# A gated delta rule on one core: inverse in packed blocks of 64, unnormalized q and k, four units of v ahead of the norm

## What is computed

```
proj = rmsnorm(x, n_mix_pre) @ w_in                 # q, k, v, z and gates of the delta rule; v of a retention
qkv  = silu(causal_depthwise_conv(concat(qa, ka, va), conv_a))       # 4 taps
qa   = l2norm(qa) * A_DK ** -0.5 ;  ka = l2norm(ka)
beta = sigmoid(beta_logit) ;  g = -exp(a_log) * softplus(a_dt + dt_bias)
lower = where(strict, (beta * k) @ k.T * decay, 0)
t_inv = inverse of (I + lower)                      # unit lower triangular, one for a chunk and head
u, w  = t_inv @ (v * beta), t_inv @ (k * beta * exp(g_cum))
o     = ...                                         # two chunks, a state of 128x256 between them
oa    = rmsnorm(o, norm_a) * silu(z)
```

## Time and profile before

| | us |
|---|---|
| median of 3 runs (1486.3 to 1490.52) | 1490.06 |
| the profiled execution | 1490.92 |
| its span, first to last instruction | 1489.4 |
| start of the layer to the first decay of head 0 | 606.9 to 646.4 |
| laps 0 to 6 | 646.4 to 975.5 |
| gate matmul with head 7 | 975.5 to 1026.1 |

### The profile page before, as it was taken

The page is one execution under the profiler, slowest core; times in us unless marked ns, Lnnn a source line. Parts: engine busy times, 40 slices in busy tenths (PEclk is TensorE's granted clock), DMA queues, the critical chain, the costliest instruction groups (busy, mean ns, idle before and its releaser), DMA issues.

```text
span 1489.4 us, 23158 instructions
## 1 busy us (share of the span) xinstructions
PE 1376.1 (92%) x9500; PEld 1249.6 (84%) x9500; DVE 940.4 (63%) x1479; ACT 730.9 (49%) x1284; POOL 89.7 (6%) x153
## 2 busy tenths in 40 slices
PE   6999999998999999868888988888999999799997
...
PEclk9999999999999999979999999999999999999998
...
GB/s 262 170 142 114 176 220 188 182 168 142 84 143 223 179 192 195 107 114 114 86 85 86 85 104 95 85 85 86 226 177 149 172 162 147 144 238 177 191 142 29
DMA packets 34057, 218.48 MB, mean 147 GB/s; under 512 B 4384, under 2 KB 6176, under 8 KB 8480
## 3 DMA queue, kind: packets, MB, share of 16 engines
...
HBM read 215.94 MB, written 1.05 MB: 146 GB/s over the span
## 4 chain that ended last, share of the span: by engine, by line
PE 75%; DVE 13%; ACT 7%; issue 3%; POOL 1%; DMA 0%; ACTq 0%; DVEq 0%; POOLq 0%
PE bank L289 22%; PE bank L290 21%; PE bank L291 21%; DVE sb_w_lo L271 3%; DVE sb_w_lo L269 2%; DVE sb_d_xt L1518 2%; ACT sb_w_hi L261 2%; PE bank L1509 1%; PE bank L1498 1%; POOL sb_small L363 1%; PE bank L708 1%; PE bank L1512 1%; ACT sb_wide L1339 1%; PE bank L397 1%; DVE sb_d_qkv_r L1346 1%
## 5 line engine op out<-in xcount | busy, mean ns | idle before, releaser
L289 PE MATMUL bank<-sb_h_hi,sb_w_hi 128*128 128x256 f32 x1536 | 445.2, 290 | 12.8 <-DVE sb_w_lo L282 7.6
L290 PE MATMUL bank<-sb_h_lo,sb_w_hi 128*128 128x256 f32 x1536 | 433.5, 282 | 0.0
L291 PE MATMUL bank<-sb_h_hi,sb_w_lo 128*128 128x256 f32 x1536 | 432.9, 282 | 0.0
L269 DVE TENSOR_TENSOR sb_w_lo<-sb_raw,sb_w_hi 128x1024 fp32r<-128x1024 f32 x199 | 242.9, 1221 | 145.4 <-ACT sb_w_hi L261 144.9
L289 PEld LDWEIGHTS bank<-sb_h_hi,sb_w_hi 128*128 128x128 f32 x1536 | 293.7, 191 | 20.1 <-issue 10.8
L290 PEld LDWEIGHTS bank<-sb_h_lo,sb_w_hi 128*128 128x128 f32 x1536 | 293.9, 191 | 2.7 <-issue 1.4
L291 PEld LDWEIGHTS bank<-sb_h_hi,sb_w_lo 128*128 128x128 f32 x1536 | 293.4, 191 | 0.0
L261 ACT CAST sb_w_hi<-sb_raw 128x1024 fp32r<-128x1024 f32 x199 | 208.8, 1049 | 85.2 <-PE bank L291 85.2
L271 DVE TENSOR_TENSOR sb_w_lo<-sb_raw,sb_w_hi 128x1024 fp32r<-128x1024 f32 x199 | 246.3, 1238 | 0.0
L262 ACT CAST sb_w_hi<-sb_raw 128x1024 fp32r<-128x1024 f32 x199 | 209.2, 1051 | 0.0
L289 PE MATMUL bank<-sb_w_hi,sb_h_hi 128*128 128x256 f32 (+1 forms) x544 | 177.9, 327 | 2.8 <-DVE sb_h_lo L431 1.4
...
## 6 DMA issues: line engine op xcount, KB each, us to landing
...
```

What stands on the lines that cost most here:

```text
L269: V.tensor_tensor(w_lo[:, b, 0:HALF], raw[:, r, 0:HALF], w_hi[:, b, 0:HALF].bitcast(F32), ALU.subtract)
L289: T.matmul(out_ap, l_hi, r_hi, start=start, stop=False, **kw)
L290: T.matmul(out_ap, l_hi, r_lo, start=False, stop=False, **kw)
L291: return T.matmul(out_ap, l_lo, r_hi, start=False, stop=stop, **kw)
```

## The change

- **Start.** Four units of v of the retention (RAW_V = 4) come first in the stream and are multiplied with the unnormalized x. Then x is normalized for good (`hn`: 8 instructions on DVE, 4 copies on ACT, 4 subtractions on DVE), and all other projections use the normalized one: `scale_qkv_dve` is gone, the convolution reads PSUM, and the scales `root` are gone elsewhere. The factor for `root` is now found from x times a gain row before the new x is made (`weighted_squares_act`). Laps 4 to 6 therefore have three units instead of four.
- **q and k.** They stay unnormalized. Their squares (ACT, one instruction, in the lap before) are summed by four matmuls with one moving column (`squares_pe`), POOL takes the power and makes scales for rows of `low`, v and k, and the scales of q go into the output's norm. Only k is transposed; `back_qk`, `scale_qk`, `norms` and `turn_low` are gone. q and k of a head have two buffers (`cv_qk`).
- **Inverse.** The two diagonal blocks of 64 of each chunk are inverted together, packed one above the other on the partitions: xt is 128x4x64 instead of 128x4x128, z 128x128 instead of 128x256. Levels 1 to 5 use 64x64 matmuls at rows 0 to 63 and 64 to 127; the corner block is then one step (`corner_a`, `corner_b`, `corner_dve`).
- **Order.** Weight work is issued in halves of a step (6 matmuls), and the small work sits at other places in all four queues.

```diff
     w = i["w_in_2"][0]
+    u += [cols_unit(w, (C_VB + 256 * h, 256)) for h in range(RAW_V)]
...
         def delta_begin_act():
...
+            hi()
+            weighted_squares_act()
...
+            hi(2)
+            keep_v_act(0)
+            keep_v_act(1)
+            row_act(7, 4)
+            for b in range(4):
+                A.wait_ge(hn_done, b + 1)
+                A.copy(h_hi[:, 2 * b:2 * b + 2, :], hn[:, 2 * b:2 * b + 2, :]).then_inc(hn_hi, 1)
+            keep_v_act(2)
             hi()
...
         def delta_begin_dve():
...
+            lo(2)
+            V.wait_ge(delta_in, DELTA_IN)
+            gates_project_dve()
...
+            V.wait_ge(row_done, 5)
+            for k in range(KD):
+                u = bank[AFTER_FFN[k // 2]][:, (k % 2) * S:(k % 2 + 1) * S]
+                ins = V.scalar_tensor_tensor(hn[:, k, :], u, gains[:, 8, k:k + 1], r_row[:], ALU.mult, ALU.mult)
...
+            for b in range(4):
+                V.wait_ge(hn_hi, b + 1)
+                V.tensor_tensor(h_lo[:, 2 * b:2 * b + 2, :], hn[:, 2 * b:2 * b + 2, :],
+                                h_hi[:, 2 * b:2 * b + 2, :].bitcast(F32), ALU.subtract).then_inc(hn_lo, 1)
+            lo(2)
...
+        def squares_pe(hd):
+
+            T.wait_ge(qk_squared, hd + 1)
+            for j in range(4):
+                mm = T.matmul(bank[2][:, 256 + j:257 + j], sq_qk[:, j * P:(j + 1) * P], upper[:, P - 1:P], start=True, stop=True)
+            mm.then_inc(ss_mm, 1)
...
+        def start_own_dve(hd):
+            V.wait_ge(blocks_done, 6 * hd + 1)
+            need(V, zx_mm, 6 * hd)
+            for s, rows in enumerate(HALF_ROWS):
+                V.tensor_tensor(xt[rows, 2:4, :], eye[rows, :].unsqueeze(1).to_broadcast([HB, NT, HB]),
+                                low_b[rows, 0, :, s * HB:(s + 1) * HB], ALU.subtract)
...
         def level_a_pe(hd, b):
-            T.wait_ge(blocks_done, 6 * hd + b)
+            T.wait_ge(blocks_done, 6 * hd + b + 1)
             T.wait_ge(inv, LEVELS * hd + b)
             for t in range(NT):
-                mm = T.matmul(bank[6][:, t * P:(t + 1) * P], low_b[:, b % 2, t, :], xt[:, t, :], start=True, stop=True)
+                for s, rows in enumerate(HALF_ROWS):
+                    mm = T.matmul(bank[6][rows, t * HB:(t + 1) * HB], low_b[rows, b % 2, t, s * HB:(s + 1) * HB], xt[rows, t, :],
+                                  start=True, stop=True)
             mm.then_inc(z_mm, 1)
...
         def delta_first_pe():
-            first_two(unit_d(0, 0), 0, unit_d(0, 1), 1, 20, 4, AFTER_FFN)
+            raw_x = (hr_hi, hr_lo)
+            first_two(unit_d(0, 2), 0, unit_d(1, 2), 1, 20, 4, AFTER_FFN, raw_x, tokens, tokens)
+            for step in range(4):
+                tokens(unit_d(2, 2), 2, step, raw_x)
+            row_pe(7, 5, R0)
+            T.wait_ge(v_ret_done, 1)
+            for step in range(4):
+                tokens(unit_d(3, 2), 0, step, raw_x)
             gates_project_pe()
...
         def delta_first_dve():
+            gates_dve()
+            lo()
             older_dve(0, 0, 1)
...
             older_dve(0, 1, 3)
...
+            new_x_dve()
...
         def delta_pe(hd):
...
+            row_decay_pe(hd)
+            T.wait_ge(v_ret_done, min(A_HEADS, RAW_V + hd))
+            T.wait_ge(conv_d[0], n)
+            head_unit_pe(u, 0, 0, 2)
+            flip_k_pe(hd)
+            squares_pe(hd)
+            products_pe(hd)
             if first:
                 first_values_pe(hd - 1)
...
+            head_unit_pe(u, 0, 6, 8)
+            start_pe(hd)
             if first:
                 outputs_pe(hd - 1)
...
         def delta_act(hd):
...
             silu_act(n, 0)
             level_a_act(hd, 2)
+            squares_qk_act(n)
             if first:
                 store_act(hd - 1)
             newest_act(n, 1)
-            hi()
             level_a_act(hd, 3)
+            if more_v:
+                hi()
             level_a_act(hd, 4)
```

More of the change, by code:

```diff
@@ L60, in constants @@
     out["upper"] = (row <= col).astype(f)
-    out["lower_strict"] = (row > col).astype(f)
     lev = []
-    for b in range(LEVELS):
+    for b in range(LEVELS - 1):
         w = 1 << b
@@ new lines, in level_b_dve, with corner_a_pe @@
+            need(V, v1_mm, hd)
+            V.tensor_tensor(xt[HALF_ROWS[0], 2:4, :], xt[HALF_ROWS[0], 2:4, :],
+                            bank[7][HALF_ROWS[0], P:2 * P].rearrange("p (a n) -> p a n", n=HB), ALU.subtract)
+            for s, rows in enumerate(HALF_ROWS):
+                ins = V.tensor_tensor(xtf[rows, :, s * HB:(s + 1) * HB], xt[rows, 0:2, :], two(bank[7][rows, 0:P]), ALU.subtract)
+            ins.then_inc(inv, 1)
+        def corner_a_pe(hd):
+            T.wait_ge(inv, LEVELS * hd + LEVELS - 1)
+            for t in range(NT):
+                mm = T.matmul(bank[6][HALF_ROWS[0], t * HB:(t + 1) * HB], low[HALF_ROWS[1], t, 0:HB], xtf[HALF_ROWS[1], t, HB:P],
+                              start=True, stop=True)
+            mm.then_inc(z_mm, 1)
@@ new lines, in corner_b_pe, with corner_dve @@
+        def corner_b_pe(hd):
+            T.wait_ge(z_done, 6 * hd + 6)
+            for t in range(NT):
+                mm = T.matmul(bank[7][HALF_ROWS[0], t * HB:(t + 1) * HB], xt[HALF_ROWS[0], 2 + t, :],
+                              z[HALF_ROWS[0], t * HB:(t + 1) * HB], start=True, stop=True)
+            mm.then_inc(zx_mm, 1)
+        def corner_dve(hd):
+            V.wait_ge(zx_mm, 6 * hd + 6)
+            V.tensor_scalar(xtf[HALF_ROWS[0], :, HB:P], two(bank[7][HALF_ROWS[0], 0:P]), -1.0, None, ALU.mult).then_inc(inv, 1)
```

661 lines of the change are left out of this document (371 added, 290 removed).

## The result

The changed kernel takes 1417.4 us (median of 4 runs, 1413.3 to 1418.0), the kernel before 1488.2 in the same comparison; the ratio is 0.952, 95% interval 0.949 to 0.955. The forecast was 1421, with a range of 1401 to 1453. The profiled execution took 1417.87 us, against 1490.92 before: 73.1 us less. Of these, 70.4 lie in the stretch that the prediction walked (606.9 to 1026.1 before, 604.6 to 953.4 now, 419.2 against 348.8 us), 2.3 ahead of it in code that the change doesn't touch, and 0.4 behind it. Ahead of the stretch the two executions differ in the clock: 13.6 us at half of it before, 6.8 now. So some 2 us of the 73 are a difference between executions and not of the change.

The account below looks back on a forecast made before the run. PE was taken as the bound, losing 11 us of each 47.4 us lap to waits, half clock and refilling. Start, laps and gate stretch summed to 350.0 us against 419.2, 69 less, giving 1421 us; range 1401 to 1453.

Parts of the forecast that it names:

- The walk: Following all engine queues from the start through the gate stretch: 350.0 us forecast against 419.2 before, 69 us less.
- gate stretch: The stretch after the laps: same content, waits of 0.8, 0.8 and 0.5 us, 39.3 us against 50.6 before.
- PE's content: PE's work in a lap: 37.2 us after the change against 36.4 before, so only lost time can be won.
- 0.36 us for a switch of shape: Extra PE cost of each 64x64 matmul group, taken from attention: 13 groups a head, 4.7 us.
- rivals 1 and 4: Inverse levels on PE: halves don't overlap, 1450 us, chance 0.17; or shape switches cost more, 1508 us, chance 0.03.
- The margins: Laps 1 to 3: each level's input is ready less than 1 us before PE needs it, so PE never stops.
- Rival 2: All heads: new waits of 2 us each, with half clock in laps 1 to 3 and gate stretch; 1451 us, chance 0.15.
- rival 5: Laps stay near 47 us because ACT or DVE stands in splits at each inverse level; about 1489 us, chance 0.03.
- wait behind `store`: Laps 4 to 6: PE waits 2.1 us for the copy of z of level 3, half clock following in half the cases.
- Rival 3: Cleaner than walked: no half clock, no wait behind `store`, shape switches at 0.3 us; 1400 us, chance 0.12.
- Lap 0: First lap: 44.3 us, including a 3.4 us idle before `start` and 3.4 us for the clock behind it.
- the chain at the head of the lap: Old lap: squares, power, scaling and splits delay the products to 11.3 us after its first row; behind a 1.0 us wait.

Follow-up runs that it names:

- e8_blocks_128: Changed kernel with the inverse back on full 128x128 matrices and six levels, everything else as changed: 1415.8 us, ratio 0.952 to the kernel before.
- e5_pass1: Changed kernel with one idle DVE pass over q and k in every head, for which PE's products wait: 1420.7 us, ratio 0.956 to the kernel before.
- e2_newest_late: Changed kernel with level 3 of laps 4 to 6 handled before the store and the next v on ACT and DVE: 1407.6 us, ratio 0.946.
- e6_pass5: Changed kernel with five idle DVE passes over q and k in every head, for which PE's products wait: 1432.0 us, ratio 0.964.
- e12_pass_bank: Changed kernel with newest_act again waiting for a DVE pass of the unit's bank, and ACT's split ahead of the copy of z: 1440.0 us, ratio 0.969.

## Why the prediction was right, and where it was not

**The walk.** The sum was 350.0 us for the stretch, measured are 348.8. It is not the work of errors that cancel in the large terms: each of laps 1 to 3, the start and lap 0 is within 0.7 us. The largest miss is the gate stretch, 1.2 us: I had put waits of 0.8, 0.8 and 0.5 us there, and PE has only 0.4 for a subtraction and 0.5 at the head of the stretch. From the profiled 1490.9 the sum gives 1421.7 us (1421 fits the median), and 1417.9 were measured: 1.2 of the difference are in the stretch, 2.7 outside of it, where nothing was changed. That second part is luck.

**PE's content.** 37.2 us were forecast for a lap; lap 3 is 38.2 with 0.7 of waits. The pair price and the 0.36 us for a switch of shape are as taken from attention, so rivals 1 and 4 are out. The 3.6 us for the levels took all 66 matmuls as paired; six of them, of the last level and the corner, have one half alone, which makes it 4.0. By the Trainium skill (TensorEngine Tiling (Array Packing), Restrictions and Gotchas) the two row halves could not have used bank 6 at the same time. The trace shows them overlapped in it, writing partitions 0 to 63 and 64 to 127: 0.58 us for a group with both halves and for one with a single half. The Trainium skill's page PSUM — Partial Sum Buffer (PSUM bank collisions raise a hardware error) reports collisions of two row tiles that write into the same bank and the same 32 partitions, which agrees with the overlap seen at different partitions; it also quotes the rule by the bank alone, and there the measurement decides.

**The margins.** I had 0.7 us of slack at each level of laps 1 to 3 after the first (17.3 against 16.6, and so on); measured are 1.0 to 1.1. That PE is never stopped is right, and e8_blocks_128 and e5_pass1 show that the slack is more than the kernel needs. Rival 2 is out in laps 1 to 3, and rival 5 with the result.

**Laps 4 to 6.** The wait behind `store` was placed rightly and comes at 1.6 us, not 2.1, and the half clock in all three laps instead of half of them: 17.0 us at half the clock in sum, 8.5 lost, where I had 5.1. The waits were 1.9 us shorter in sum than forecast and the clock cost 3.4 more: 112.5 us against 111.0, so part of the agreement is luck. Rival 3, no wait and no half clock, is what e2_newest_late then made: 33.6 us a lap.

**Lap 0.** 3.4 us were forecast before `start`, 2.4 were measured and 0.6 before level 1; the 1.4 for the silu and squares of k came as 1.2, and of the 2.6 us of smaller waits behind them only those 0.6 did. The clock is at half for 10.2 us instead of 6.8. Again errors of opposite sign, 3.2 us of waits too many (7.4 against 4.2) and 1.7 of clock too few, with 0.8 that no row accounts for, leave 0.7: luck for this lap.

**The old half clock.** The prediction says 6.8 us at half the clock in each steady lap. Lap 4 of the old kernel had 3.4 and took 46.2 us. It changes no term of the sum, since the new laps were added up from content.

**The step that failed** is not one of the sum but of the reasons. Under "Other engines" I costed the two multiplications with r_row as 1.4 us of DVE's time and nothing on the path. Under "What bounds the kernel now" I gave a cause, the chain at the head of the lap, for the last and smallest of the three waits only (1.0 us). For the 2.3 and 1.7 us rival 5 alone names one, ACT and DVE standing in splits, which is half of what was found; the expectation of e6_pass5 then laid all of them on the chain. The experiments say: the chain, put back in part, gives a wait of 0.8 us and is worth 1.2 us a lap; the dependence of `newest_act` on DVE, with the split ahead of the copy, gives 2.0 and is worth 2.8; the order of PE 0.7; the packing -0.5. The forecast came out right because the walk laid all queues of the new kernel side by side and never needed to know what had held up the old one.

**What stays open** is the half clock of the old laps. Waits of 2.0 us in lap 3 of e12_pass_bank leave the clock full, the old kernel's 2.3 and 0.9 close together were followed by 6.8 us at half, and in laps 4 to 6 the same waits are followed by it in one lap and not in another. Over the whole execution it was 102.6 us of the old kernel and is 51.3 of the new one. In the stretch that the change touches it was 71.5 us, in 11.5 of which PE had nothing to do, and is 27.2; half of the difference of the rest, 16.4 us, is what it gave of the 70.4. No edit brought it back into laps 1 to 3. The runs show that it goes with the waits but not at which one it begins, and other executions of the old kernel, at a mean granted clock of 0.972 instead of 0.966, had less of it.
